# Retention scores of two heads in the two row halves of TensorE, every second slab, and two fp32 products ahead of the third FFN's wide products

## What is computed

```python
    def step(state, inp):
        qi, ki, vi = inp
        scores = jnp.einsum('bhnd,bhmd->bhnm', qi, ki) * inner_decay
        out = (jnp.einsum('bhnm,bhme->bhne', scores, vi)
...
def swiglu_ffn(x, w_gate, w_up, w_down):
    return (jax.nn.silu(x @ w_gate) * (x @ w_up)) @ w_down
```

## Time and profile before

| what | value |
|---|---|
| median of 3 runs | 1352.17 us (1351.78 to 1352.49) |
| the profiled execution | 1351.47 us |
| its span | 1349.7 us |
| TensorE products busy | 1314.5 us (97%) |
| VectorE busy | 869.8 us (64%) |
| ScalarE busy | 617.6 us (46%) |
| GpSimd busy | 110.5 us (8%) |
| DMA | 224.82 MB, mean 167 GB/s |
| mean granted TensorE clock | 0.992 |

### The profile page before, as it was taken

How to read it: one execution, slowest core, us unless ns; L and a number is a source line. 1 busy time by engine, 2 the same in 40 slices (tenths; PEclk the granted TensorE clock), 3 DMA queues, 4 the chain that set the end, 5 groups by cost and what they waited for, 6 DMA issues and landing times.

```text
span 1349.7 us, 17758 instructions
## 1 busy us (share of the span) xinstructions
PE 1314.5 (97%) x7338; PEld 1133.4 (84%) x7338; DVE 869.8 (64%) x966; ACT 617.6 (46%) x745; POOL 110.5 (8%) x148
## 2 busy tenths in 40 slices
PE   7999999999999999997999999999999989999997
PEld 5878877888888888996988888998888877988886
DVE  5555676767666655876677755566665556676653
ACT  5354576534455433215355543445553445455540
POOL 4123111001000002130000000000000101100000
PEclk9999999999999999998999999999999989999999
DMA  9644544456655655400656564556555521566550
GB/s 312 163 154 156 173 140 149 164 187 196 209 186 189 217 189 176 124 2 22 198 182 192 194 213 158 185 167 207 187 188 187 187 94 60 175 192 191 194 172 32
DMA packets 164911, 224.82 MB, mean 167 GB/s; under 512 B 7473, under 2 KB 105857, under 8 KB 164832
## 3 DMA queue, kind: packets, MB, share of 16 engines
q1 hardware_dynamic: 163168, 220.23, 50.7%
q0 software_dynamic: 1648, 3.47, 1.0%
q10 hardware_dynamic: 16, 0.00, 0.0%
HBM read 222.62 MB, written 1.05 MB: 166 GB/s over the span
## 4 chain that ended last, share of the span: by engine, by line
PE 95%; DVE 3%; ACT 1%; DMA 1%; issue 0%; POOL 0%; SPq 0%; POOLq 0%; DVEq 0%; ACTq 0%
PE acc L587 15%; PE acc L589 15%; PE acc L588 15%; PE acc L644 14%; PE att L644 8%; PE acc L642 7%; PE att L877 4%; PE att L642 4%; PE acc L622 2%; PE acc L618 2%; PE acc L620 2%; PE tp L665 1%; DVE wlo L1291 1%; DMA raw<-in_w_in_dram 1%; DVE wexp L1808 0%; ACT whi L1017 0%
## 5 line engine op out<-in xcount | busy, mean ns | idle before, releaser
L1291 DVE TENSOR_TENSOR wlo<-raw,whi 128x2048 fp32r<-128x2048 f32 x208 | 474.4, 2289 | 171.5 <-ACT whi L1017 171.4
L1017 ACT ACTIVATE whi<-raw 128x2048 fp32r<-128x2048 f32 x208 | 394.8, 1913 | 105.8 <-PE acc L589 94.0
L644 PE MATMUL acc<-aT,whi 128*128 128x512 f32 x832 | 292.3, 393 | 0.0
L642 PE MATMUL acc<-aT,wlo 128*128 128x256 f32 x832 | 233.7, 281 | 0.0
L587 PE MATMUL acc<-whi,aT 128*128 128x512 f32 x480 | 192.9, 402 | 8.8 <-DVE aT L1724 6.2
L588 PE MATMUL acc<-whi,aT 128*128 128x512 f32 x480 | 189.2, 394 | 0.0
L589 PE MATMUL acc<-wlo,aT 128*128 128x512 f32 x480 | 189.2, 394 | 0.0
L644 PEld LDWEIGHTS acc<-aT,whi 128*128 128x128 f32 x832 | 155.8, 187 | 35.0
L644 PE MATMUL att<-aT,whi 128*128 128x512 f32 x448 | 158.5, 393 | 0.0
L642 PEld LDWEIGHTS acc<-aT,wlo 128*128 128x128 f32 x832 | 157.2, 189 | 0.0
L587 PE MATMUL acc<-whi,hT_hi 128*128 128x512 f32 x352 | 137.3, 390 | 0.0
(11 more groups left out here) (281 smaller groups left out, 1682.6 us busy)
## 6 DMA issues: line engine op xcount, KB each, us to landing
raw<-in_ffn_w_gate_dram SPq DMA_DIRECT2D x88, 512.0 KB, 4.1
raw<-in_ffn_w_up_dram SPq DMA_DIRECT2D x88, 512.0 KB, 5.2
raw<-in_ffn_w_down_dram SPq DMA_DIRECT2D x88, 512.0 KB, 4.8
raw<-in_w_in_dram SPq DMA_DIRECT2D x72, 512.0 KB, 4.7
raw<-in_conv_w_pw_dram SPq DMA_DIRECT2D x24, 512.0 KB, 4.7
raw<-in_w_kv_dram SPq DMA_DIRECT2D x16, 512.0 KB, 4.9
raw<-in_ret_w_o_dram SPq DMA_DIRECT2D x8, 512.0 KB, 4.6
raw<-in_diff_w_o_dram SPq DMA_DIRECT2D x8, 512.0 KB, 4.7
```

What stands on the lines that cost most here:

```text
L642: mm_(bank[:, 0:T], wlo[:, slot, cols], aT_hi[:, kt, :], start=half == 0 and j == 0, stop=False, skip_group_check=True)
L644: last = mm_(bank[:, :], whi[:, slot, cols], aT[:, kt, :, :].rearrange("p a n -> p (a n)"), start=False, stop=half == 1 and j == SLAB_K - ...
L1017: A_(whi[:, slot, :], raw[:, slot, :], ACT.Copy).then_inc(hi_ready, 1)
L1291: V.tensor_tensor(wlo[:, slot, :], raw[:, slot, :], whi[:, slot, :].bitcast(F32), ALU.subtract)\
```

## The change

It has two parts. The scores of retention are issued for two heads at once, behind slabs 9, 11, 13 and 15, and there behind the output; the products of the two heads alternate, as in stick-breaking attention. And the third FFN gets two fp32 products of `ones` with `ones` behind s = 2, into tp[0], whose result nobody reads.

```diff
                     if s == 2 and name in SPREADS:
                         spread_rs(name, tp[0])
+                    elif s == 2:
+                        for _ in range(TT):
+                            mm_(tp[0][:, 0:P], ones[:, :], ones[:, :], start=True, stop=True)
...
-            def score(bank, lhs, rhs, base, dk):
-
-                pr = slice(base, base + dk)
-                mm_(bank[:, 0:T], lhs[pr, 0:P], rhs[pr, :], start=True, stop=True)
-                return mm_(bank[:, T:3 * P], lhs[pr, P:T], rhs[pr, P:T], start=False, stop=True,
-                           skip_group_check=True)
+            def ret_scores(m):
+
+                parts = [slice(RDK * e, RDK * (e + 1)) for e in range(2)]
+                for e, pr in enumerate(parts):
+                    mm_(att[e][:, 0:T], qkT_r[pr, 4 + m, 0:P], qkT_r[pr, m, :], start=True, stop=True)
+                for e, pr in enumerate(parts):
+                    mm_(att[e][:, T:3 * P], qkT_r[pr, 4 + m, P:T], qkT_r[pr, m, P:T], start=False, stop=True,
+                        skip_group_check=True).then_inc(r_score, 1)
...
-                if RET0 <= s < RET0 + RH:
-                    i = s - RET0
-                    if i == 0:
-                        pe.wait_ge(rt_done, 4)
-                    if i >= 2:
-                        pe.wait_ge(r_prob, i - 1)
-                    score(att[i % 2], qkT_r[:, 4 + i // 2, :], qkT_r[:, i // 2, :], RDK * (i % 2), RDK)\
-                        .then_inc(r_score, 1)
                 if RET0 < s <= RET0 + RH:
                     i = s - RET0 - 1
                     pe.wait_ge(r_prob, i + 1)
...
+                if RET0 <= s < RET0 + RH and (s - RET0) % 2 == 0:
+                    i = s - RET0
+                    if i == 0:
+                        pe.wait_ge(rt_done, 4)
+                    else:
+                        pe.wait_ge(r_prob, i)
+                    ret_scores(i // 2)
```

## The result

The changed kernel takes 1344.72 us, the median of 5 runs (1342.52 to 1346.16), against 1352.06 us for the kernel before (5 runs, 1350.90 to 1352.49). The ratio is 0.9947 with a 95% interval of [0.9936, 0.9959], so 5.5 to 8.7 us faster. The forecast was 1346.5 with a range of 1345.4 to 1348.6: the direction is right, the time lies 0.7 us under the range, and the runs spread over 3.6 us where the five of before spread over 1.6 (24 later runs of before spread over 3.9). The gain forecast, 5.7 us, lies inside the interval; it is the median that fell outside the range.

A forecast was written before the change was run, and what follows sets the result against it. TensorE's own sequence was taken as the bound (95% of the chain that ended last). Part one's 4.14 us plus part two's 1.57 gave 5.71, so 1352.17 - 5.71 = 1346.5 us, with a range of 1345.4 to 1348.6.

The forecast's parts named there:

- The pair at 0.85 us: Retention: scores of two heads issued together hold TensorE 0.85 us, as much as one head's scores before.
- the slabs with an output alone at 6.17: Retention slabs 10, 12, 14 and 16 take 6.17 us each, together saving 4.05 us.
- no wait on the decays: Retention: TensorE does not wait on attT at the outputs; the 0.2 us left at head 2's decay counted as nothing.
- the 5.54 of the earlier trace: Retention: a slab's own products behind an output take 5.54 us, read from slab 17 before the change.
- The unproven premise that the two row halves run over each other: Retention: products of the two halves overlap, so a pair costs 0.85 us; without overlap the upper bound is 1.50.
- The 0.98 us estimated from the Trainium skill's 3.07 times for four tiles: Retention: alternative pair cost with imperfect overlap, 0.13 us more per pair, 0.5 us over four pairs; not used in the sum.
- which kind of instruction came last before the run: Third FFN: this sets the wide products' rate for the whole run, so two fp32 products save 1.57 us.
- The rival that the wide products stay slow with ones times ones: Third FFN: products of ones leave the slow rate and cost 0.36 us; gain 3.78, time 1348.4 us; 8%.
- the one without overlap: Retention: the pair's halves do not overlap, 0.65 us for each of four pairs; gain 3.1, time 1349.1 us; 6%.
- the slow rate behind the pairs: From slab 10 on, pairs leave later slabs slow, costing up to 7.3 us; with part two failing 1355.7 us; 2%.
- The step that failed: Behind retention, DMAs, loads and halves of work depend on TensorE's progress and move with it, so the gain stays whole.
- the term for run to run differences: Whole kernel: 0.35 us to either side of the median before, giving 1345.6 to 1347.2 with tenths in entries.

The follow-up runs named there:

- samehalf: Changed kernel with both heads' score operands taken from the same row half, so odd heads' own scores are left out; 1344.85 us in one run.
- p1: Kernel before with the paired retention scores alone, without the two fp32 products in the third FFN; 1347.56 us, ratio 0.9975.
- p2: Kernel before with the two fp32 products in the third FFN alone, retention scores as before; 1349.57 us, ratio 0.9990.
- again: The changed kernel unaltered, timed once more beside new runs of before; 1345.20 us, ratio 0.9954.
- afill: Changed kernel with unread fp32 products of ones filling TensorE's long waits at the convolution's end and in stick-breaking attention; 1340.76 us, ratio 0.9930.
- probes2: Changed kernel without the third FFN's two products, with unread fp32r and fp32 products put among wide slabs of the second, third and fourth FFNs; 1354.58 us, one run.
- bfill: Kernel before with unread fp32 products of ones filling TensorE's long waits at the convolution's end and in stick-breaking attention; 1346.99 us, ratio 0.9973.

## Why the prediction was wrong

**Part one** held by its steps. The pair at 0.85 us (0.85 and 0.86 measured), the slabs with an output alone at 6.17 (6.18 and 6.16), no wait on the decays: 3.95 us gained instead of 4.14. The difference lies mostly in slabs 11, 13, 15 and 17, whose own products take 5.57 to 5.58 us behind an output where I had carried over the 5.54 of the earlier trace rows, 0.14 us in all; the next slab of that trace, 129.69 to 135.27, had shown 5.58. The unproven premise that the two row halves run over each other is shown by `samehalf`, 1.50 against 0.85. The 0.98 us estimated from the Trainium skill's 3.07 times for four tiles ("TensorE: Matmul & The Clock Gate", on packing small matmuls) is not what this trace gives for two tiles, 0.85 and 0.86.

**Part two** held to the hundredth: 1.57 us. The reason named, "which kind of instruction came last before the run", was right in this kernel and too narrow in general: two fp32r products behind wide ones at 173.5 ns change nothing, and a half-row fp32r product does what fp32 does. The rival that the wide products stay slow with ones times ones is out, and so is the one without overlap. So is the slow rate behind the pairs: slabs 10 to 18 take 5.57 to 5.59 us for their own products, and no time was added up to the convolution.

**The step that failed** is the sentence "Behind the stage the DMAs, loads and halves of work hang on TensorE's own progress, nothing on a fixed time, so they move with it", and with it the term for run to run differences, sized from three runs of before as 0.35 us to either side, where 24 runs of before spread over 3.9 us and 11 of the changed kernel over 4.6 (1342.52 to 1347.14). What did not move with TensorE's work is where its granted clock is low. It falls behind the waits at the convolution's end and in stick-breaking attention, and when it falls and how long it stays low differ between executions: 10.9 and 4.6 us into the two stretches in before, 8.6 and 6.7 in the changed kernel. In the traces the convolution's end takes 31.44 us in before, 31.97, 31.54, 32.08 and 31.67 in the changed kernel, `p1`, `p2` and `again`, and stick-breaking attention 39.39, 38.20, 39.43, 36.89 and 38.20, without a change in either. With the waits filled it is 30.05 and 35.51 (`afill`). So 3.4 to 5.4 us of each time hang on this (1.7 in `samehalf`), where the prediction had the clock only as a mean of 0.992 in the table and did not ask where it was low. Of the 7.3 us measured, 5.5 are the change's own (the stretches). The other 1.8 us (0.6 in `again`) I put down to the granted clock: the changed kernel's runs at 0.995 are the shortest of both sets, and the trace of `samehalf` at 0.995 is shorter in just these two stretches.

Why the changed kernel sometimes gets more clock and `p1` and before never did is open. One guess was that part two brings the second wait 1.5 us nearer to the first, where part one moves both by the same 4 us. `probes2` speaks against it: its second stretch begins 487.4 us behind its first (611.35 to 1098.77, 479.7 in the changed kernel), and it had 0.995 and 37.04 us in stick-breaking attention all the same. No experiment moved one wait alone.

The rule of the Trainium skill that bears on the low stretches ("TensorE: Matmul & The Clock Gate", on the clock gate) is the one by which the engine's clock falls when it has been idle; the filled kernels agree (0.95 and 1.00 in `bfill`, 1.00 twice in `afill`, where it was 0.84 to 0.91 in before and changed).

## What to carry to other kernels

Two products with at most 64 contraction rows cost as much as one when they lie in different row halves (and, here, in different banks, which was not varied); issue them together, also where this puts one head's scores a slab early. A long run of equal products may have a slow and a fast rate, set by what stands ahead of it; compare the same code at several places of one trace before believing a rate. And before forecasting a few microseconds, look at where the granted clock is low: such stretches differ from run to run, so they widen the range, and filling the idle time there (here with 42 small products) was worth 3.9 us in the kernel before, against the 5.5 of the change's own stretches.

## What the runs showed of the hardware that was not expected

- The rate of wide fp32r products is 173.5 or 176.7 ns and stays over 608 products; one fp32 product, or one fp32r product of 128 columns over 64 rows, sets the fast one, 12 or 48 fp32r products of 256 columns the slow one, 2 neither.
- Two row halves overlap fully also when the products are issued head by head: 0.86 us against 0.85 alternating and 1.50 in one half.
- With TensorE's waits filled, the clock did not fall in stick-breaking attention, where its mean had been 0.87 over 39 us (`bfill`, `afill`), nor at the convolution's end in `afill` (0.89 over 31 us in before); in `bfill` it still fell there, with no wait longer than 1.4 us ahead of it in that stretch.
- In stick-breaking attention the same work took 39.4, 38.2 or 36.9 us, with the clock at its lower level for 10, 7 or 3 us.
